# One fp32 model block on one core: norm sums laid out with tokens in partitions, a second norm taken from sums over the old h, stages that open with four weight units

## The reference, cut to what matters

```python
h = x
y = rmsnorm(h, g)*(1+sc1)+sh1;  h = h + 0.5*g1*rmsnorm(swiglu(y), post_g)     # ffn1
y = rmsnorm(h, g)*(1+sc2)+sh2;  h = h + g2*rmsnorm(token_mix(y), post_g)      # mix
y = rmsnorm(h, g)*(1+sc3)+sh3;  h = h + 0.5*g3*rmsnorm(swiglu(y), post_g)     # ffn2
h = h + gate*gla_mixer(norm(h));   h = h + gate*mlp(norm(h))                  # gla, mlp0
h = h + gate*diff_mixer(norm(h));  h = h + gate*mlp(norm(h))                  # diff, mlp1
return rmsnorm(h, final_g)
```

## Time and profile before

| | |
|---|---|
| median of 3 runs | 2452.21 us (2451.02 to 2453.96) |
| the profiled execution, its own time | 2453.7 us |
| its span | 2451.9 us |
| granted TensorE clock, mean | 0.985 of full |
| busy: PE, DVE, ACT, POOL | 98%, 52%, 34%, 7% |

### The profile page before, as it was taken

The page is one execution under the profiler, slowest core; times in us unless marked ns, Lnnn a source line. Parts: engine busy times, 40 slices in busy tenths (PEclk is TensorE's granted clock), DMA queues, the critical chain, the costliest instruction groups (busy, mean ns, idle before and its releaser), DMA issues.

```text
span 2451.9 us, 26976 instructions
## 1 busy us (share of the span) xinstructions
PE 2401.3 (98%) x10976; PEld 1913.7 (78%) x10976; DVE 1265.9 (52%) x1845; ACT 827.8 (34%) x1228; POOL 169.9 (7%) x146
## 2 busy tenths in 40 slices
PE   8999999999999999999999999999999989999998
PEld 7888887877777888887688878888867767888886
DVE  5654544476233455443534467665366664644343
ACT  3332223423433322222453343323234443433221
POOL 0000002021012000001101100000111211000001
PEclk8999999999999999999999999999999999999999
DMA  7756542311112256642232136664121212343330
GB/s 282 258 187 210 190 124 72 93 51 44 60 49 63 86 169 210 199 142 61 87 95 78 52 106 213 205 206 151 56 99 52 61 52 69 117 133 95 95 95 34
DMA packets 80793, 288.06 MB, mean 117 GB/s; under 512 B 8976, under 2 KB 9104, under 8 KB 80672
## 3 DMA queue, kind: packets, MB, share of 16 engines
q1 hardware_dynamic: 79952, 284.78, 36.7%
q10 hardware_dynamic: 720, 1.57, 0.2%
HBM read 284.22 MB, written 2.10 MB: 117 GB/s over the span
## 4 chain that ended last, share of the span: by engine, by line
PE 92%; DVE 4%; ACT 1%; POOL 1%; issue 1%; DMA 0%; DVEq 0%; SPq 0%; POOLq 0%; ACTq 0%
PE bank L275 25%; PE bank L277 24%; PE bank L276 24%; PE bank L362 2%; PE bank L318 1%; PE bank L295 1%; PE bank L320 1%; PE bank L319 1%; PE bank L391 1%; PE bank L296 1%; PE bank L369 1%; PE bank L300 1%; PE bank L712 1%; PE bank L408 1%; POOL h_sb L1957 1%; PE bank L351 1%
## 5 line engine op out<-in xcount | busy, mean ns | idle before, releaser
L275 PE MATMUL bank<-yhi,whi 128*128 128x512 f32 x1808 | 719.9, 398 | 6.8 <-DVE ylo L1556 6.4
L277 PE MATMUL bank<-yhi,wlo 128*128 128x512 f32 x1808 | 708.4, 392 | 0.0
L276 PE MATMUL bank<-ylo,whi 128*128 128x512 f32 x1808 | 708.3, 392 | 0.0
L1349 DVE TENSOR_TENSOR wlo<-raw,whi 128x1024 fp32r<-128x1024 f32 (+1 forms) x370 | 464.1, 1255 | 431.5 <-ACT whi L844 431.1
L844 ACT ACTIVATE whi<-raw 128x1024 fp32r<-128x1024 f32 (+1 forms) x370 | 384.8, 1041 | 328.3 <-PE bank L277 261.9
L275 PEld LDWEIGHTS bank<-yhi,whi 128*128 128x128 f32 x1808 | 342.1, 189 | 98.4 <-issue 23.6
L277 PEld LDWEIGHTS bank<-yhi,wlo 128*128 128x128 f32 x1808 | 342.0, 189 | 72.5
L276 PEld LDWEIGHTS bank<-ylo,whi 128*128 128x128 f32 x1808 | 342.4, 189 | 69.0 <-issue 0.7
L277 PE MATMUL bank<-mlp_ahi,wlo 128*128 128x512 f32 x512 | 204.2, 399 | 0.0
L276 PE MATMUL bank<-mlp_alo,whi 128*128 128x512 f32 x512 | 201.8, 394 | 0.0
L275 PE MATMUL bank<-mlp_ahi,whi 128*128 128x512 f32 x512 | 200.8, 392 | 0.0
(11 more groups left out here) (292 smaller groups left out, 2440.9 us busy)
## 6 DMA issues: line engine op xcount, KB each, us to landing
raw<-in_ada SPq DMA_DIRECT2D x152, 512.0 KB, 4.3
raw<-in_ffn_up SPq DMA_DIRECT2D x88, 512.0 KB, 4.4
raw<-in_mlp_up SPq DMA_DIRECT2D x64, 512.0 KB, 3.6
raw<-in_mlp_dn SPq DMA_DIRECT2D x64, 512.0 KB, 3.7
raw<-in_ffn_dn SPq DMA_DIRECT2D x32, 512.0 KB, 3.7
raw<-in_w_dqkv SPq DMA_DIRECT2D x24, 512.0 KB, 3.6
first<-in_ada SPq DMA_DIRECT2D x16, 512.0 KB, 15.9
raw<-in_ffn_dn SPq DMA_DIRECT2D x16, 384.0 KB, 3.6
```

The source lines that it names most:

```text
L275: e.matmul(out, wh, xh[:, kt, :], start=first, stop=False)
L276: e.matmul(out, wh, xl[:, kt, :], start=False, stop=False)
L277: mm = e.matmul(out, wl, xh[:, kt, :], start=False, stop=last)
L1349: e.tensor_tensor(k.wlo[:, what % NW, 0:width], raw[:, 0:width], k.f(k.whi[:, what % NW, 0:width]), ALU.subtract).then_inc(*sig.up("wlo", ...
```

## The change

It has five parts. (1) All norm sums are made the other way round: the squares are the weights and a single column of ones moves (`column`), so tokens lie in partitions and the sums in 4 columns by 128 partitions; root and reciprocal then work on 128x4 and `spread` loads the column as weights. The heads' norms, the mLSTM's denominators and their roots go the same way. (2) `postnorm` is gone. While the last units run, ACT also squares the scaled output z (`cz`) and DVE multiplies z by the old h (`hz`), POOL adds all three kinds, and TensorE sums them (`bridge`); the sum over the new h is then worked out from the old one by five small DVE operations, so both roots follow each other before h itself is updated. (3) mix, ffn2, gla, mlp0, diff and mlp1 open with four units in step, each tile kt doing eight products with `yhi` and then four with `ylo`. (4) Shifts 4 to 7 of ffn1 are made by DVE (`ada(0, n)`), shifts 1 and 2 come before `four`. (5) diff puts 12 slices ahead of the attention, moves others, and gets five warm-up matmuls near its end. The new `prep_to(self.u + NW - 2)` stands in ACT's and DVE's programs before the last tile of a stage. The diff, cut:

```diff
 # Pe
+    def four(self, tags, x, hi, before=None):
         us = [self.count(tag) for tag in tags]
         outs = [self.bank("u", u) for u in us]
+        for n in range(NT + (3 if before else 0)):
+            for kt, group in ((n, us[0:2]), (n - 3, us[2:4])) if before else ((n, us),):
...
+                w.wait_ge(*sig.on(hi, *st, kt))
+                for u in group:
+                    w.wait_ge(*sig.on("wlo", u))
+                    out = outs[u - us[0]]
+                    e.matmul(out, k.whi[:, u % NW, c], xh[:, kt, :], start=kt == 0, stop=False)
+                    e.matmul(out, k.wlo[:, u % NW, c], xh[:, kt, :], start=False, stop=False)
                 w.wait_ge(*sig.on(lo, *st, kt))
+                for u in group:
+                    mm = e.matmul(outs[u - us[0]], k.whi[:, u % NW, c], xl[:, kt, :], start=False, stop=kt == NT - 1)
+    def column(self, out, col, sq, first, last):
         for j in range(4):
+            mm = self.e.matmul(out[:, col + j:col + j + 1], sq[:, 128 * j:128 * j + 128], self.k.one,
+                               start=first and j == 0, stop=last and j == 3)
+    def bridge(self, st):
+        w.wait_ge(*sig.on("sqadd", st, 6))
+        self.column(out, 0, k.tm(4), True, False)
+        w.wait_ge(*sig.on("hzadd", st, 6))
+        self.column(two, 0, k.tm(0), True, False)
+        w.wait_ge(*sig.on("czadd", st, 6))
+        self.column(two, 4, k.tm(6), False, False)
+        w.wait_ge(*sig.on("sq", st, 7))
+        self.column(out, 0, k.tm(5), False, True).then_inc(*sig.up("tot", st))
+        w.wait_ge(*sig.on("hz", st, 7))
+        self.column(two, 0, k.tm(1), False, False)
+        w.wait_ge(*sig.on("cz", st, 7))
+        self.column(two, 4, k.tm(7), False, True).then_inc(*sig.up("tot", "two", st))
+        self.warm(1)
+        self.root(st, 0)
+        self.warm(1)
+        self.w.wait_ge(*sig.on("rrow", st + "h"))
+        self.spread(("R", st + "h"), k.rs, 4)
+        self.warm(1)
 # Act
+    def four(self, tags):
+        us = [self.count(tag) for tag in tags]
+        self.prep_to(us[0] + NW)
+        return us
     def prenorm(self, st, sums, v_shift):
-        self.prep_to(self.u + NW - 1)
-        self.root(sums)
+        if sums[-1] == "h":
+            self.root(sums[:-1])
+            w.wait_ge(*sig.on("ssum", sums[:-1]))
+            self.e.activation(k.rs[:, 4:8], k.rs[:, 8:12], k.ACT.Sqrt, ...)
+        else:
+            self.prep_to(self.u + NW - 1)
+            self.root(sums)
         for n in range(NT):
             w.wait_ge(*sig.on("scaled", st, n))
...
+                    if n == NT - 1:
+                        self.prep_to(self.u + NW - 2)
 # Dve (its four() is as ACT's)
+    def bridge(self, st, nx, z, g, v_shift, v_scale):
...
+        self.root(st + "h")
+        w.wait_ge(*sig.on("spread", "R", st))
+        post(0)
+        post(1)
+        e.tensor_tensor(k.h[:, 0, :], k.h[:, 0, :], k.tm(0)[:, 0:S], ALU.add).then_inc(*sig.up("hv", st, 0))
         for n in range(NT):
+            if n + 2 < NT:
+                post(n + 2)
+            scaled(n)
+            if n:
+                low(n - 1)
+        low(7)
 # Pool
+    def bridge(self, st):
+        for n in range(1, 7):
+            for kind, total in (("sq", 4), ("hz", 0), ("cz", 6)):
...
+        for n in range(1, NT):
             w.wait_ge(*sig.on("post", st, n))
+            self.e.tensor_tensor(k.h[:, n, :], k.h[:, n, :], k.tm(n)[:, 0:S], ALU.add).then_inc(*sig.up("hp", st, n))
```

More of the change, by code:

```diff
@@ L388, in spread @@
+    def spread(self, key, cols, col):
         e, k = self.e, self.k
@@ L399, in root @@
         self.w.wait_ge(*self.sig.on("rrow", st))
-        self.spread(("R", st), self.k.total_row, 0, 4)
+        self.spread(("R", st), self.k.rs, 0)
         if warm:
             self.warm(warm)
[L404 to L410, removed]
     def ffn(self, st, counts, gated):
@@ L418, in up @@
             done = 0
+            if g == 0:
+                done = 4
+                self.four([tag] * 4, y, "yhi", self.shift_ahead if st == "ffn1" else None)
             if st == "ffn1" and g == 0:
-                self.four(tag, y, self.shift_ahead)
                 for i in range(3):
                     k.banks.let_go(("shift", i))
[L423 to L426, removed]
             for _ in range(done, n):
@@ L497, in mix @@
         y = (k.yhi, k.ylo, "ylo", ("mix",))
-        self.pair(["mif", "hq"], y, "yhi")
-        for _ in range(3):
-            self.linear("hq", y)
+        self.four(["mif", "hq", "hq", "hq"], y, "yhi")
+        self.linear("hq", y)
         for _ in range(4):
@@ L622, in mix @@
             self.linear("wout", x, order)
-        self.totals_end("mix")
+        self.bridge("mix")
     def gla(self):
@@ L627, in gla @@
         y = (k.yhi, k.ylo, "ylo", ("gla",))
-        self.pair(["ga", "gq"], y, "yhi")
-        for _ in range(3):
-            self.linear("gq", y)
+        self.four(["ga", "gq", "gq", "gq"], y, "yhi")
+        self.linear("gq", y)
         for i in range(4):
@@ L679, in diff, with part @@
         y = (k.yhi, k.ylo, "ylo", ("diff",))
-        self.pair(["dqkv", "dqkv"], y, "yhi")
+        self.four(["dqkv"] * 4, y, "yhi")
+        first = self.u - 4
+        outs = {}
+        def part(n, kt, x=y):
+            u = first + n
+            xh, xl, lo, st = x
+            if kt == 0:
+                outs[u] = self.bank("u", u, hold=True)
+            w.wait_ge(*sig.on("wlo", u))
+            w.wait_ge(*sig.on(lo, *st, kt))
+            self.three(outs[u], u, kt, xh, xl, kt == 0, kt == 7)
+            if kt == 7:
+                k.banks.let_go(("u", u))
         def turn(n):
@@ L937, in up @@
                 tag, first = f"{st}_up{g}", (g, i) == (0, 0)
-                if first and st == "ffn1":
-                    self.two = [self.count(tag) for _ in range(4)]
-                    self.prep_to(NW)
-                elif first:
-                    self.two = self.pair([tag, tag])
+                if first:
+                    self.two = self.four([tag] * 4)
                 u = self.two.pop(0) if self.two else self.unit(tag)
@@ L1613, in mix @@
         w.wait_ge(*sig.on("lbd", 6))
-        self.pair(["mif", "hq"])
-        for _ in range(3):
-            self.unit("hq")
+        self.four(["mif", "hq", "hq", "hq"])
+        self.unit("hq")
         for i in range(4):
```

538 lines of the change are left out of this document (288 added, 250 removed).

## The result

The change makes the kernel slower: 2516.27 us median (2510.52 to 2518.35, 4 runs) against 2451.62 (2451.02 to 2453.96, 4 runs), ratio 1.0258 with a 95% interval of 1.024 to 1.0277. The profiled execution took 2518.35 us with a span of 2516.5, 64.6 more than the span before. The forecast was 2495 and its range reached to 2516. The direction and the main mechanism came as forecast; the size came out at the very end of the range, with a change half as large again as forecast (64.6 against 43).

What follows compares the result with a forecast made beforehand. TensorE, busy 98% of 2451.9 us, was taken as the bound. Bridges and ffn2 28.5, mlp stages 18.2, diff 2.7, start -3 and reciprocals -1.6 sum to +44.8, giving 2497, trimmed to 2495 us; range 2464 to 2516.

Steps and rivals of the forecast that it cites:

- Bridges, mechanism: At three seams: the fourth unit is prepared late, so TensorE stalls 13 to 18 us six matmuls into `four`.
- Bridges, size: Three seams up to the fifth unit: each bridge loses 8.6, three 25.8, and mix 1.8 more.
- it is worse: Rival, bridges: column sums drop the clock, +1.8 each, or POOL's adds block lows, up to +6.6 each; 2502 to 2517, chance 0.19.
- mlp0 and mlp1: Opening with four: waits for low(0) 1.7, fifth unit 2.0, sixth 4.0, plus clock; 9.1 each, 18.2 in all.
- the 1.7 of clock: mlp0 and mlp1: after the sixth unit's wait the clock starts low, costing 1.7 us of work.
- the sixth unit's share: mlp0 and mlp1: the sixth unit, prepared after four hidden tiles, costs +4.0 of wait and +1.7 of clock per stage.
- diff: diff's opening: new waits and clock loss, less the turned keys' wait filled by 12 slices; +2.7.
- The tail: End of diff: fewer slices, preparation two steps earlier, five warm-ups; taken as 0, bounds -6 and +6.
- What is left of the stages: Outside openings: reciprocals in mix and at the end shorten by 0.76 each, -1.6; ffn2's sixth unit costs +0.9.
- The start: Up to ffn1's first units: four shifts leave TensorE and DVE sets the pace; -3, bounds -8 and +2.
- The warning that one-column work might run at half speed: Start: some column sums, shift 0 and the spread run at half speed, putting DVE back 1 to 4.
- The upper bound of 8.5 a bridge: Bridges: if each low waits for a whole POOL add, 8.5 instead of 1.9 a bridge, 2515 in all.

Runs made afterwards that it cites:

- run 1: Changed kernel with ScalarE and VectorE preparing the next stage's fourth weight unit at the head of each bridge; 2457.79 us.
- run 10: Changed kernel with GpSimd's adds to h in the bridges cut to one column of 512; 2505.7 us.
- run 5: Changed kernel with the sixth to eighth unit of mlp0 and mlp1 prepared one by one ahead of the first three hidden tiles; 2507.02 us.
- run 12: Kernel with the edits of run 1, run 2 and run 3 together, plus twelve slices ahead of diff's step 0 behind the old opening; 2423.11 us.
- run 6: Changed kernel keeping diff's new opening and twelve slices, the other 148 slices spread over 28 steps and the tail as before; 2501.68 us.
- run 3: Changed kernel with diff's schedule as before (opening, slices, output weights, no warm-ups), the new norm sums kept; 2496.94 us.
- run 8: Kernel with the edits of run 1, run 2 and run 3 together, with the start as before, all eight shifts on TensorE; 2419.42 us.
- run 9: Kernel with run 1, run 2 and run 3 together, plus a warm-up among each bridge's column sums and four units as two pairs one tile apart; 2424.82 us.
- run 2: Changed kernel with mlp0 and mlp1 opened by a pair of units again; 2496.37 us.
- run 11: Changed kernel without the five warm-ups around the last two spreads in diff's tail; 2509.86 us.

## Why the prediction was right, and where its sizes were off

**Bridges, mechanism: right.** The stall inside `four` after six matmuls, ended by wlo, whi after the eighth `yhi`, at three seams; two lines at the right place remove it (run 1). From the resumption to the fifth unit 24.95 us were forecast; 24.4, 25.1 and 24.7 were measured.

**Bridges, size: +40.3 instead of +27.6.** One microsecond of the miss is the kernel before, whose fifth unit began at 44.3 and not at 44.7. The rest lies before the resumption, forecast at 30.2 in mix and 28.4 at the others, measured at 31.9, 34.6 and 32.6. Two terms were mis-sized. The lows beside GpSimd's adds were put at 0.3 each for five and one add, 1.9 in all; they lost 3.2 (one 0.87, four 0.57), and removing the adds gave 3.0 back (run 10); VectorE's row took 19.9 where 18.9 were forecast. The larger one is the column sums. I had six tiles at 0.93, 5.6 us, at the full clock. In mix they took 5.7. In the bridge to ffn2 the last four took this, after a wait of 1.1 for GpSimd's longer row of sums, and the stretch ran at 0.54:

```profile
783.45 1.84 PE L372 MATMUL bank<-cst,tmps 128*128 128x1 f32 x16
786.41 6.99 PE L372 MATMUL bank<-cst,tmps 128*128 128x1 f32 x32 [1.13 <-POOL tmps L2067]
...
795.11 1.53 PE L420 MATMUL bank<-cst,rs 128*128 128x128 f32 x8
```

```profile
785.00:795.00 10.00, 8.87 (x37) 7.86 (x37) 3.17 (x10) 1.80 (x4) 1.36 (x1) 0.54 0.19 54
```

The first spread ended at about 13 there instead of 7.8, at 11 in the bridge to gla, at 9 in that to mix. This was the rival "it is worse", priced at 1.8 a bridge; it came true beside the forecast, not in its place. That the total still fell at the end of the range is partly luck: the bridges and diff cost 25 more than forecast, and 8 came back in stretches where the forecast had nothing.

**mlp0 and mlp1: right, term by term.** 18.2 forecast, 17.9 measured. The waits are 1.6, 1.9 and 3.7 where 1.7, 2.0 and 4.0 were forecast; behind them the clock stood at 0.50 for 3.4 us, the 1.7 of clock. Run 5 takes out the sixth unit's share, 9.5 of the 11.4 forecast for it in both stages.

**diff: the step that failed.** The opening was put at +2.7. Up to the first scores it lost 3.9, near enough; but the 12 slices were booked as a gain (they fill the wait for the turned keys), and nothing was booked for the steps that then have fewer. Run 12 shows that exchange. The tail was put at 0 with bounds of 6 on both sides; with the spacing it cost 10.2, outside them. Waits in all are not the reason: those for ylo are 7.4 with the new tail and 7.8 with the old one (run 6). What differs is what lies around them. In the changed kernel TensorE waits 1.05, 1.38 and 7.41 us between 2060 and 2071, with six short matmuls between, and from 2062.45 the clock stands at half speed for 17 us, 9.06 of them busy; with run 6's longest wait, 5.42, it does so for 6.8, 4.47 of them busy. First the changed kernel, then run 6:

```profile
2062.45:2079.51 17.06, 9.06 (x27) 6.32 (x28) 8.36 (x19) 5.01 (x11) 0.00 (x0) 0.50 0.21 62
```

```profile
2057.49:2064.32 6.83, 4.47 (x11) 3.52 (x12) 5.52 (x14) 1.98 (x8) 0.00 (x0) 0.50 0.22 77
```

So the 10.2 are 1.2 of idle time, 4.6 of warm-ups and 4.4 of clock. Which of the new steps brings the waits so close together was not tested: the spacing and the preparation's step were not run apart.

**What is left of the stages: better than forecast.** I counted two reciprocals, 1.6. mix behind its fifth unit gained 7.0, gla 2.3, diff 5.6 (run 3), and ffn2 lost 1.6. In mix the wait for the root's reciprocal fell from 1.9 to 0.8 and the mLSTM's four spreads from 4.98 to 3.84; the rest of that gain was not tested apart.

**The start: the step failed, and the number is luck.** The forecast took 4 us off VectorE's path, to a last low part done at 53.7, and gave back 1. The column sums took 11.5 us in the changed kernel's profile where the row sums took 7.15, the last low part was done at 60.1 (58.1 before), and ffn1 ended 0.4 earlier. In nine of twelve profiles it ended 3.5 earlier, close to the forecast, but not by the shifts as far as the runs show: with the old shifts and sums just as long it ends no later (run 8; the old shifts were not seen with the short sums). What else shortened ffn1 is open. The warning that one-column work might run at half speed was in the prediction; it was underpriced.

The Trainium skill, "SBUF — State Buffer", section "Who interferes with whom", holds that a VectorE instruction with two SBUF inputs and a GpSimd one that reads SBUF exclude each other, while VectorE with one SBUF input goes free. The rows agree: scaled tiles, one input in a bank, took 0.73 beside the same adds, lows 1.31. But a low lost 0.57, not a whole add of 1.26: it began 0.5 into the add (432.87 against 432.36). The upper bound of 8.5 a bridge was too high.

## What to carry to other kernels

When a stage's head is rewritten, check each preparation that the old head made as a side effect, and whether the index in a new call names a unit that isn't made yet: here two missing calls cost 57 us, and with them the three bridges gain 16 on the kernel before. Start more units together only where the operand is made more slowly than two units consume it, and then count the unit behind them: all slots come free at once. Work taken from a covered stretch to fill a wait has to be priced in both places.

## What the hardware showed that was not expected

TensorE's clock fell from 2.4 to 1.2 GHz while TensorE was busy without a gap, in matmuls with one moving column: from 9 to 20 us it was busy 11.00 of 11.00 in both kernels, at a granted clock of 0.75 with column sums and of 1.00 with row sums (128 moving columns), and from 20 to 30 the changed kernel stood at 0.50, busy 10.00 of 10.00 (run 8). 64 such matmuls took 8.6 to 9.3 or 11.0 to 11.5 us in different executions of kernels that are alike there, and ffn1 ended 3 us later with the longer ones. A single warm-up of 1.1 us among 48 sums didn't keep the clock (run 9).

The same kernel's runs lie up to 11.5 us apart (run 1: 2455.64 to 2467.15), so steps of 1 to 3 us were judged by stage lengths in the traces. These vary too. In the profiles of kernels that are alike up to the end of gla (the changed kernel and runs 2, 3, 5, 6 and 11) mix took 374.6 to 377.5 us, ffn2 398.8 to 402.5 and gla 261.9 to 263.6; diff, where its code is the same, took 312.4 to 312.5.
